# Two token buffers move by 32 bytes in each partition of SBUF

## The reference, cut to what matters

```python
xn = rmsnorm_2(x, norm_mix[l])
(qa, ka, va, qb, kb, vb, qc, kc, vc, qi, ki, wi, gates) = jnp.split(xn @ w_in[l], offsets, axis=-1)
...
y = (g[:, :, 0] * (o_a @ w_up_a[l]) + g[:, :, 1] * (o_b @ w_up_b[l])
     + g[:, :, 2] * (o_c @ w_up_c[l]))
x = x + y @ w_out[l]
x = x + memory_cross_attention(rmsnorm_2(x, norm_cross[l]), mem_n, w_q_x[l], w_kv_x[l], w_o_x[l])
g, u = jnp.split(rmsnorm_2(x, norm_ffn[l]) @ w_gu[l], 2, axis=-1)
x = x + (jax.nn.silu(g) * u) @ w_down[l]
```

## Time and profile before

| What | Value |
|---|---|
| time, median of 3 runs | 1655.73 us |
| the three runs | 1655.55, 1655.73, 1657.57 us |
| span of the profiled execution | 1656.0 us |
| PE busy | 1580.1 us, 10,931 matmuls |
| PEld busy | 1274.8 us |
| DVE busy | 908.4 us |
| ACT busy | 651.3 us |
| POOL busy | 63.5 us |
| mean granted TensorE clock | 0.984 |

### The profile page before, as it was taken

The page is one execution under the profiler, slowest core; times in us unless marked ns, Lnnn a source line. Parts: engine busy times, 40 slices in busy tenths (PEclk is TensorE's granted clock), DMA queues, the critical chain, the costliest instruction groups (busy, mean ns, idle before and its releaser), DMA issues.

```text
span 1656.0 us, 25664 instructions
## 1 busy us (share of the span) xinstructions
PE 1580.1 (95%) x10931; PEld 1274.8 (77%) x10931; DVE 908.4 (55%) x1302; ACT 651.3 (39%) x1022; POOL 63.5 (4%) x30
## 2 busy tenths in 40 slices
PE   8988989899889999999999999999999999999998
PEld 7876434334344459888899799999989889899998
DVE  5943212112121158678886576647667879476654
ACT  2034112112111144454654554435454664464443
POOL 0000000000000000043000000000006000000000
PEclk9988999999999999999999999999999999999999
DMA  9165999999999995735242556474633643275550
GB/s 350 39 254 208 421 427 429 429 427 429 429 428 428 426 369 183 231 109 179 102 153 102 189 168 203 153 258 156 213 119 108 217 153 128 87 227 172 177 202 28
DMA packets 126913, 393.79 MB, mean 238 GB/s; under 512 B 4320, under 2 KB 60000, under 8 KB 114016
## 3 DMA queue, kind: packets, MB, share of 16 engines
q1 hardware_dynamic: 126816, 392.38, 62.6%
HBM read 386.34 MB, written 1.05 MB: 234 GB/s over the span
## 4 chain that ended last, share of the span: by engine, by line
PE 70%; DVE 15%; DMA 11%; issue 2%; ACT 2%; SPq 0%; DVEq 0%; ACTq 0%
PE psum L1260 11%; PE psum L991 9%; DMA ring<-w 9%; PE psum L994 9%; PE psum L992 9%; PE psum L1325 3%; DVE outs L1985 3%; PE psum L1595 2%; PE psum L1598 2%; PE psum L1597 2%; DVE w_lo L637 2%; PE psum L1223 2%; DVE score L2383 1%; PE psum L1022 1%; PE psum L952 1%
## 5 line engine op out<-in xcount | busy, mean ns | idle before, releaser
L991 PE MATMUL psum<-h_hi,w_hi 128*128 128x256 f32 x1472 | 366.2, 287 | 1.6 <-DVE w_lo L637 1.6
L992 PE MATMUL psum<-h_hi,w_lo 128*128 128x256 f32 x1472 | 360.7, 283 | 0.0
L991 PEld LDWEIGHTS psum<-h_hi,w_hi 128*128 128x128 f32 x1472 | 281.9, 192 | 7.5 <-issue 7.1
L637 DVE TENSOR_TENSOR w_lo<-raw_a,w_hi 128x1024 fp32r<-128x1024 f32 x184 | 221.6, 1222 | 116.5 <-ACT w_hi L1617 115.8
L992 PEld LDWEIGHTS psum<-h_hi,w_lo 128*128 128x128 f32 x1472 | 282.1, 192 | 0.2
L1617 ACT ACTIVATE w_hi<-raw_a 128x1024 fp32r<-128x1024 f32 x202 | 210.3, 1053 | 167.8 <-PE psum L994 68.9
L994 PE MATMUL psum<-h_lo,w_hi 128*128 128x256 f32 x1472 | 206.4, 283 | 0.0
L1260 PE MATMUL psum<-ring,outs 128*64 128x512 f32 x720 | 166.7, 619 | 26.4 <-DMA ring<-w 25.2
L994 PEld LDWEIGHTS psum<-h_lo,w_hi 128*128 128x128 f32 x1472 | 189.9, 192 | 0.0
L1260 PEld LDWEIGHTS psum<-ring,outs 128*64 128x64 f32 x720 | 57.9, 143 | 132.4 <-issue 132.0
L1617 ACT ACTIVATE w_hi<-raw_b 128x1024 fp32r<-128x1024 f32 x100 | 104.6, 1054 | 94.9 <-PE psum L994 56.0
(11 more groups left out here) (311 smaller groups left out, 2560.7 us busy)
## 6 DMA issues: line engine op xcount, KB each, us to landing
ring<-w SPq DMA_DIRECT2D x76, 2048.0 KB, 16.6
raw_a<-w_in SPq DMA_DIRECT2D x20, 2048.0 KB, 8.6
raw_a<-w_gu SPq DMA_DIRECT2D x32, 1024.0 KB, 7.8
raw_b<-w_in SPq DMA_DIRECT2D x10, 2048.0 KB, 8.9
wp<-w SPq DMA_DIRECT2D x8, 2048.0 KB, 18.3
hs<-w SPq DMA_DIRECT2D x8, 2048.0 KB, 22.7
raw_b<-w_gu SPq DMA_DIRECT2D x12, 1024.0 KB, 7.1
raw_a<-w_down SPq DMA_DIRECT2D x8, 1536.0 KB, 6.7
```

The costliest lines, as they stand in the source:

```text
L637: return eng.tensor_tensor(chunk_part(w_lo, n), chunk_raw(n), chunk_part(w_hi, n).bitcast(F32), ALU.subtract)
L991: mm(to, hi[:, k, :], h_hi[:, k, :], start=(k == 0), stop=False)
L992: mm(to, lo[:, k, :], h_hi[:, k, :], start=False, stop=False)
```

## The change

`h_hi` and `h_lo` become two views of one tensor `h_parts`, which begins where `h_hi` began and has 8 elements (32 bytes) unused ahead of the tokens and 8 behind. So the tokens stand 32 bytes later, and every tensor behind them 64 bytes later. The 64 bytes come from `side` and `eps2`, two columns of 4 bytes that took 32 bytes each and now are columns 4 and 5 of `lam`, whose columns 0 to 3 alone were used.

```diff
+H_SHIFT = 8
...
-        h_hi = sb("h_hi", [P, KD, SEQ], F32R)
-        h_lo = sb("h_lo", [P, KD, SEQ], F32R)
+        h_parts = sb("h_parts", [P, 2 * KD * SEQ + 2 * H_SHIFT], F32R)
+        h_hi, h_lo = (view(h_parts, H_SHIFT + i * KD * SEQ, KD, SEQ) for i in range(2))
...
-        side = sb("side", [P, 1])
-        eps2 = sb("eps2", [P, 1])
+        side, eps2 = lam[:, 4:5], lam[:, 5:6]
```

## The result

The kernel after takes 1667.46 us, median of 5 runs (1661.74 to 1668.23), beside 1655.73 us before (5 runs, 1655.04 to 1657.57). The ratio is 1.0055 with a 95% interval of 1.0044 to 1.0066: slower by half a per cent, where 0.4% less was forecast. Repeated in ten runs of the same file it gave 1664.45 us, ratio 1.0035 [1.0008, 1.0062]. The profiled execution of after is the shortest of the first five: span 1659.7 us, 3.7 us above the 1656.0 of before.

A forecast was written before the change was run, and what follows sets the result against it. The prediction took PE's price per matmul to bound the layers and the weight stream the experts' stage. Its terms, -6.9 - 0.3 + 0.5 = -6.7 us, took 1655.7 to 1649.0 us, range 1643 to 1658 us.

The forecast's parts named there:

- What bounds the kernel: In the layers the price of one matmul on PE decides, times some 4,300; in the experts' stage the DMA stream.
- The price of 1.6 ns: Token matmuls on the chain, 4,310 of them, go from 119.9 to 118.3 ns each: -6.9 us.
- the remainder by 64: Each matmul costs 1.6 ns more when moving operand and weights loaded beside it have the same address remainder by 64 bytes.
- Rival B: 5 ns less for each of 5,490 matmuls, 27 us in all, giving 1628 us; chance 0.10.
- the 13 ns: Time around each 256-column matmul beyond its columns' 107 ns; if all went, the gain would be 56 us.
- The value projections: 192 matmuls with the tokens as the loaded side gain the same 1.6 ns each: -0.3 us.
- What moves by 64 bytes: Tensors behind the tokens: no change taken; bad end +1.6 us if the 990 `act_parts` matmuls lose 1.6 ns each.
- What is not on the chain: PE's saving is worth nothing where DVE alone is the chain, including where it picks the top keys.
- the attention stretches: The chain hops between PE and DVE; of 2.5 us gain there, 0.5 us was taken as lost.
- Rival D: The new place is worse: token and `act_parts` matmuls go to 121.5 ns, 10.4 us slower, 1666 us; chance 0.08.
- PE saves its 7 us and gaps behind DVE or ACT give them back: A listed sign that the prediction is wrong: PE's gain is lost to waits on the other engines.
- The first layer: A listed sign of success: this layer ends 3 to 4 us earlier, with the experts' stage unmoved.

The follow-up runs named there:

- gated pair: The kernels before and after, each with POOL waiting for DVE's first L2391 ahead of its sixth chunk of a layer: 1657.43 and 1642.9 us.
- the tokens at 64 and 96: Kernel after with the tokens 64 or 96 bytes behind their old place and POOL waiting for the first L2391: 1648.23 and 1659.77 us.
- behind_only: Kernel after with the tokens left at their old place, everything behind them still moved by 64 bytes: 1656.96 us, ratio 1.0005.
- the two kernels at 64: Kernel after with the tokens 64 bytes behind their old place: 1648.23 us with POOL waiting for the first L2391, 1668.99 us without.
- gated after: Kernel after with POOL waiting for the first L2391 ahead of its sixth chunk of a layer: 1642.9 us, ratio 0.9924 to before.
- after_again: Kernel after without an edit, repeated in ten runs on the same chip: 1664.45 us.
- 6 and 24 increments: Kernel after with 6 or 24 unused semaphore increments on DVE ahead of each layer's first L2391: 1668.56 us (one run) and 1664.56 us.
- gated before: Kernel before with POOL waiting for the first L2391 ahead of its sixth chunk of a layer: 1657.43 us, ratio 1.0006.

## Why the prediction was wrong

- **What bounds the kernel.** Right: PE's price per matmul decides. With the wait taken away, the change is worth 14.5 us in the gated pair.
- **The price of 1.6 ns.** The sign was right and the size half of it: 3.1 ns per token matmul, by the means over the whole execution 119.9 to 116.8 (the 100 us window alone has 116.7). The price was borrowed from `act_parts` at another place, and the table shows that it doesn't carry over. The reading behind it, the remainder by 64, is refuted by the tokens at 64 and 96. Rival B had more of the 13 ns go; of its 5 ns, 3.1 came.
- **The value projections.** -0.3 us was forecast and +1.2 us came (192 x 6.0 ns): with the tokens as the loaded side the sign is the opposite.
- **What moves by 64 bytes.** Nothing was forecast, and as a whole it is nothing (`behind_only`). The 990 matmuls of `act_parts` gained 1.6 us in after; that case was not among my bounds, which had a loss only. Their move alone gave a third of that (117.8 ns in `behind_only`), and the two kernels at 64 show that their interval hangs on more than the place.
- **What is not on the chain.** This is the step that failed. I wrote that what PE saves where DVE picks the top keys "is worth nothing", and took +0.5 us for the attention stretches, at worst the 2.5 us of gain lost. It cost 9.4 + 9.0 = 18.4 us. I priced the loss of a gain, but not that an earlier PE could make an instruction of DVE longer. The rows for it were there to read: L2391 as 756 ns for a mask of 128 x 128, and L2383 as 2.39 us beside POOL's chain, both too long for their size, so DVE was already queueing for POOL at that place. They are not among my rows.
- **The rest of the attention stretches.** In gated after, 612 to 853 and 1134 to 1371 us gave 2.4 us together; the full price would have been 188 / 0.1199 x 3.07 ns = 4.8 us less the 1.2 us of the value projections, 3.6 us. The loss was 1.2 us where 0.5 was taken, at a price twice as large.
- **Rival D.** It had the sign and not the way. Its intervals above 120.2 ns never came; the slowdown came with faster matmuls. "PE saves its 7 us and gaps behind DVE or ACT give them back" stood among the signs that I would be wrong, and it is what happened, with 18.4 us of gaps.
- **The first layer** was to end 3 to 4 us earlier with the experts unmoved. At 1134 us after stands at -0.4 + 1.6 = +1.2 us against its own start of the layers, gated after at -9.1.

Open: the profiled execution of after is at 1661.7 us and most others are at 1665 to 1668. The runs list a mean granted clock for each: 0.976 for the profiled one and 0.972 to 0.975 for the four others; in `after_again` the two at 1652 us have 0.979 and 0.980, and those above 1666 us 0.972 to 0.974. 0.004 of 1660 us are 6.6 us of clock, about the 5.7 us between 1661.74 and the median. The profiled executions with 6 and 24 increments, spans 1666.4 and 1666.3 us, have further dips than after. I take it that the missing microseconds are such dips, but no profile of after itself shows one of these runs, so this is argued. It is also unseen whether L2391 has its long wait in the runs at 1652 us. By an estimate it has only one of the two there: 1661.7 less the 9.4 us of one wait is 1652.3 us, and they took 1652.2 and 1652.3. If so, the same kernel at the same pace sometimes gets in, and neither pace nor place settles it alone.

## What to carry to other kernels

Before costing a faster engine, list the instructions of the other engines at that place that last longer than their size explains (here 0.76 us for 0.23 us of work): they already wait for something that no semaphore shows, and a shift can make that wait many times longer. Where GpSimd runs a chain without a pause beside VectorE work that the critical path needs, put a wait on GpSimd ahead of one link of the chain; it held GpSimd for 0.3 us here and gave back 9 us in each layer. Where float32r matmuls bound a kernel, the place of the operands by 128 bytes is worth a sweep of four runs. Each place has to be measured with the stationary and the moving use apart, and in each stage, since one tensor at one place had 116.7 ns in one layer and 120.0 in the next.

## What the hardware showed that I had not expected

- An instruction of DVE waited through the rest of one and five more instructions of POOL, 12.7 us, and got through only at a pause of 0.27 us; the same instruction, arriving at the same point (1696 and 1699 ns), got through after one with the tokens at their old place and PE at its old pace. Both forms of it do so. With the tokens at 64 it got through after the rest of one and four more, without a pause. What decides is open, and whether it is the pace of PE or the place of the tokens too. How early ACT has the next chunk ready doesn't decide (1.8 us where DVE got in, 2.0 to 0.3 us where it lost). The rest of the traffic of ACT and of the DMAs I did not test.
- The interval of the token matmuls (float32r, 256 columns) is 119.9, 116.8, 117.7 and 120.0 ns with the moving operand at 0, 32, 64 and 96 bytes by 128; with 512 columns and the same tensor as the loaded side it is 227.3, 233.3, 233.3 and 234.1 ns. With `act_parts` as the moving operand at 32 it is 116.7, 117.8 or 120.0 ns, two of them in one execution. What lies behind it is open.
- The same gap of 1.85 us in PE's work is followed by a granted clock of 0.50 in one kernel and of 1.00 in another. Where such dips differ, a stretch differs by 1.1 to 2.9 us (1440 to 1455 us: +1.1 in after, +2.9 in `after_again`; 925 to 945 us: -1.9 in gated before).
- 24 semaphore increments on DVE held it for 2.28 us before L2391 (some 90 ns each):

```profile
740.89 10.51 DVE L2393 TENSOR_SCALAR wp<-score 128x128 f32<-128x128 f32 x1 [2.28 <-issue]
```
